# A two-block transformer forward pass on one core: query norm factors of the attention heads move into the exponential, squares of the low-rank parts are added on GpSimd, and sixteen modulation quarters move from TensorE to VectorE

## The reference, cut to what matters

```python
def rms(x, w):
    y = xf * lax.rsqrt(jnp.mean(xf * xf, axis=-1, keepdims=True) + EPS)
    return (y * w).astype(x.dtype)
...
qa = rms(heads(qa, H_A), qn_a)          # 8 heads of 64
ka = rms(heads(ka, H_A), kn_a)
qb = rms(heads(qb, H_B), qn_b)          # 12 heads of 64
kb = rms(heads(kb, HKV_B), kn_b)        # 4 heads of 64
qc = rms(heads(rms(cq, qa_norm) @ w_qb, H_C), qn_c)     # cq has 768 columns
kvc = heads(rms(ckv, kva_norm) @ w_kvb, H_C)            # ckv has 512 columns
...
qb, kb = apply_rope2d(qb, cos, sin), apply_rope2d(kb, cos, sin)   # latent tokens
...
s = einsum(q, k) * D ** -0.5 (+ bias for heads a, mask and sink for heads b)
p = softmax(s); o = p @ v
```

## Time and profile before

| what | value |
|---|---|
| median of 3 runs | 3268.7 us (3268.28 to 3268.73) |
| the profiled execution's own time | 3265.98 us |
| its span, first to last instruction | 3264.2 us |
| busy share PEld / DVE / ACT / POOL | 85% / 70% / 44% / 21% |
| DMA of the weight stream | 534.60 MB, queue 1 |
| FFN | about 810 to 1618 us |
| stages a0, za0, b0, zb0, c0 | from 1643, 1785, 1888, 2006, 2152 us |
| stages a1, za1, b1, zb1, c1 | from 2640, 2751, 2805, 2889, 2969 us |

### The profile page before, as it was taken

One profiled execution on the slowest core, in us unless ns is written; L12 is line 12 of the kernel. 1 busy time (PEld: TensorE's weight loads), 2 busy tenths in 40 slices (PEclk: granted clock), 3 DMA queues, 4 the chain that ended last, 5 costly groups with the idle time before them and its releaser, 6 DMA issues.

```text
span 3264.2 us, 56041 instructions
## 1 busy us (share of the span) xinstructions
PE 3220.0 (99%) x20212; PEld 2763.4 (85%) x20212; DVE 2299.4 (70%) x3399; ACT 1429.2 (44%) x2193; POOL 669.2 (21%) x600
## 2 busy tenths in 40 slices
PE   8999999999999999999999999999999999999999
PEld 8999999998998777889888777777878888888878
DVE  7887877567786776777766766566658776776765
ACT  5444445445444343444543433532352363543453
POOL 4999930111450000000300011000001100210000
PEclk9999999999999999999999999999999999999999
DMA  6555555565577777777733222134316553324435
GB/s 220 182 181 185 184 184 187 184 211 187 194 246 258 250 254 256 248 253 244 256 105 113 102 92 83 53 135 140 105 65 213 199 175 113 133 97 142 154 102 177
DMA packets 159873, 559.71 MB, mean 171 GB/s; under 512 B 17552, under 2 KB 23840, under 8 KB 159264
## 3 DMA queue, kind: packets, MB, share of 16 engines
q1 hardware_dynamic: 154144, 534.60, 48.1%
q0 software_dynamic: 5504, 22.04, 2.0%
HBM read 550.26 MB, written 6.31 MB: 171 GB/s over the span
## 4 chain that ended last, share of the span: by engine, by line
PE 89%; DVE 5%; ACT 2%; issue 1%; DVEq 1%; ACTq 0%; DMA 0%; POOL 0%; POOLq 0%; SPq 0%
PE psum L2168 17%; PE psum L2172 17%; PE psum L2169 17%; PE psum L2195 15%; PE psum L2196 7%; PE psum L2379 3%; PE psum L2521 2%; PE psum L2547 2%; PE psum L2532 2%; PE psum L2224 2%; PE psum L2380 2%; DVE wlo L1332 1%; PE psum L2299 1%; DVE rst L1363 1%; DVEq L1318 1%
## 5 line engine op out<-in xcount | busy, mean ns | idle before, releaser
L1332 DVE TENSOR_TENSOR wlo<-raw,whi 128x1024 fp32r<-128x1024 f32 (+3 forms) x844 | 1037.0, 1235 | 379.7 <-ACT whi L866 348.9
L866 ACT ACTIVATE whi<-raw 128x1024 fp32r<-128x1024 f32 (+3 forms) x844 | 863.3, 1029 | 949.9 <-PE psum L2172 465.3
L2168 PE MATMUL psum<-hcat,whi 128*128 128x256 f32 (+1 forms) x3436 | 1122.7, 327 | 4.9 <-DVE wlo L1332 4.2
L2172 PE MATMUL psum<-hcat,wlo 128*128 128x256 f32 (+1 forms) x3436 | 1109.4, 323 | 0.0
L2169 PE MATMUL psum<-hcat,whi 128*128 128x256 f32 (+1 forms) x3436 | 1109.3, 323 | 0.0
L2195 PE MATMUL psum<-hcat,whi 128*128 128x512 f32 x2048 | 724.2, 397 | 0.1
L2168 PEld LDWEIGHTS psum<-hcat,whi 128*128 128x128 f32 x3436 | 653.2, 190 | 72.9 <-issue 16.1
L2172 PEld LDWEIGHTS psum<-hcat,wlo 128*128 128x128 f32 x3436 | 653.1, 190 | 51.4
L2169 PEld LDWEIGHTS psum<-hcat,whi 128*128 128x128 f32 x3436 | 653.5, 190 | 49.4 <-issue 0.7
L2196 PE MATMUL psum<-hcat,wlo 128*128 128x256 f32 x2048 | 573.3, 280 | 0.0
L2195 PEld LDWEIGHTS psum<-hcat,whi 128*128 128x128 f32 x2048 | 384.3, 188 | 105.9 <-issue 17.2
(11 more groups left out here) (307 smaller groups left out, 3647.3 us busy)
## 6 DMA issues: line engine op xcount, KB each, us to landing
raw<-in_stream SPq DMA_DIRECT2D x978, 512.0 KB, 3.9
raw<-in_stream SPq DMA_DIRECT2D x18, 384.0 KB, 3.0
raw<-in_stream SPq DMA_DIRECT2D x24, 256.0 KB, 2.9
resid_dram<-X POOLq DMA_DIRECT2D x2, 2048.0 KB, 9.4
crow<-c_dram POOLq DMA_DIRECT2D x4, 1024.0 KB, 9.1
bias<-in_natten POOLq DMA_DIRECT2D x16, 256.0 KB, 2.9
X<-resid_dram POOLq DMA_DIRECT2D x4, 1024.0 KB, 6.2
raw<-in_stream SPq DMA_DIRECT2D x16, 192.0 KB, 2.4
```

Source lines behind the costliest of these rows:

```text
L866: act.activation(whi[:, c % HI_SLOTS, 0:n], raw[:, slot, 0:n], ACT.Copy).then_inc(hi_ready, 1)
L1332: vec.tensor_tensor(wlo[:, slot, 0:n], raw[:, slot, 0:n], whi[:, c % HI_SLOTS, 0:n].bitcast(F32), ALU.subtract).then_inc(lo_ready, 1)
L2168: pe.matmul(dst, h, cat[:, kk, c0:c0 + width], start=(q == 0 and k == 0), stop=False)
L2172: last = pe.matmul(dst, l_, cat[:, kk, c0:c0 + width], start=False, stop=(q == nq - 1 and k == nch - 1))
```

## The change

1. **Query factors.** The jobs of the query tiles of heads a and b are gone. Each query tile is squared once by ACT (`q_square`; for b straight from PSUM), and PE makes column sums with the square as the stationary side: 4 full float32 matmuls of two columns in layer 0, 2 in layer 1 (`qcol`, before tile t + 2). Once a stage, `q_factors` on DVE makes from all of them the factors for the exponential and for the maximum. The product of the gains of query and key goes into the keys (heads a); for heads b the query gain is applied as the tile leaves PSUM, which waits for ACT's square. Bias (heads a) is now scaled per head, two instructions instead of one; heads b have one small instruction more before the exponential. The key jobs stay, and the sum of layer 1's stage a stands one tile earlier.
2. **Rope of heads b** is done by DVE alone.
3. **Low-rank squares.** ACT squares one tile at a time, POOL adds them (`lora_adds`), and PE sums one source for ckv and two for cq.
4. **Modulation.** The last two FFN groups lose their eight quarters among the down tiles (`MOD_FEWER`): 16 quarters, two blocks. They come as rows of stage a0 (two beside each of tiles 0 to 3) and b0 (two beside tiles 0, 1, 4, 5). The second half of the vector is then loaded after the first four quarters of b0.

```diff
-MOD_GROUPS = [MOD_FEW] * FF_GROUPS
+MOD_FEWER = [0, 2] * 8 + [0] * KD
+MOD_GROUPS = [MOD_FEW] * 3 + [MOD_FEWER] * 2
...
-ROW_MODS = dict(a0=[0] * 10 + [1, 1], za0=[1] * 6, c0=[2, 2, 0, 2, 2, 2, 1, 1, 2, 1, 1])
+ROW_MODS = dict(a0=[2, 2, 2, 2, 0, 0, 0, 0, 0, 0, 1, 1], za0=[1] * 6, b0=[2, 2, 0, 0, 2, 2, 0, 0, 0, 0], c0=[2, 2, 0, 2, 2, 2, 1, 1, 2, 1, 1])
...
+            def heads_at(js, nq_):
+                for t in range(nq_):
+                    at_(t + 1, "qsq", t)
+                    at_(t + 2, "qcol", t)
+                    if name == "b":
+                        at_(t + 1, "rope", ROPES_OF[f"b{l}"][t])
+                at_(nq_ + 2, "qstat")
...
-                at_(4, "sq", ckv, 0, 4, 3)
-                at_(5, "sum", ckv, 0, 4)
+                for m in range(4):
+                    at_(m + 1, "part", ckv, m, l, m)
+                at_(5, "sum", ckv, 0, 1)
...
-                at_(9, "sq", cq, 0, 3, 7)
-                at_(10, "sum", cq, 0, 3)
-                at_(k0, "sq", cq, 3, 6, 10)
-                at_(k0 + 1, "sum", cq, 3, 6)
+                for m in range(6):
+                    at_(6 + m, "part", cq, m, l, 5 + m)
+                at_(k0, "sum", cq, 0, 1)
+                at_(k0 + 1, "sum", cq, 1, 2)
...
+            def q_factors(name, l):
+                k, nq_ = 2 * l + (name == "b"), Q_TILES[name]
+                st = q_mean(nq_, l)
+                nb = chunks_w(l) // P
+                vec.wait_ge(qsq_used, q_no(name, l, nq_))
+                sums_ = psum[:, 6, 0:8 * nq_].rearrange("p (h b) -> p h b", b=4)[:, :, 0:nb]
+                vec.tensor_scalar(st, sums_, 1.0 / HD, EPS, ALU.mult, ALU.add).then_inc(q_mean_ready, 1)
+                vec.wait_ge(q_root_ready, k + 1)
+                if name == "a":
+                    vec.tensor_scalar(q_inverse[:, :, :], st[:, :, 0:2], HD ** 0.5, None, ALU.mult)
+                    fence()
+                vec.reciprocal(st, st)
+                fence()
+                for dst, f in ((q_factor, HD ** -0.5), (q_minus, -HD ** -0.5)):
+                    vec.tensor_scalar(dst[:, 0:2 * nq_, 0:nb], st, f, None, ALU.mult)
+                fence()
...
-                    vec.scalar_tensor_tensor(ps[:, :, 0:S], bias[:, n % BIASES, :, :], 1.0 / u["scale"], ps[:, :, 0:S],
-                                             ALU.mult, ALU.add)
+                    for h in range(2):
+                        vec.scalar_tensor_tensor(ps[:, h, 0:S], bias[:, n % BIASES, h, :],
+                                                 q_inverse[:, 2 * u["c"] + h, u["q0"] // P:u["q0"] // P + 1],
+                                                 ps[:, h, 0:S], ALU.mult, ALU.add)
...
+                    elif it[0] == "qcol":
+                        name, t = "b" if first == T0[f"b{l}"] else "a", it[1]
+                        n = q_no(name, l, t)
+                        pe.wait_ge(qsq_ready, n + 1)
+                        for b in range(chunks_w(l) // P):
+                            last = pe.matmul(psum[:, 6, 8 * t + b:8 * t + b + 8:4], sq[:, n % 4, P * b:P * b + P],
+                                             halves[:, 0::HD], start=True, stop=True)
+                        last.then_inc(qsq_used, 1)
...
+            def lora_adds(l, name, j):
+                a0, adds = LORA_ADDS[name]
+                acc, w = jobs[j]["srcs"][0][0], jobs[j]["width"]
+                for m in range(1, adds + 1):
+                    a = 7 * l + a0 + m - 1
+                    pool.wait_ge(part_ready, 9 * l + (0 if name == "ckv" else 4) + m + 1)
+                    pool.tensor_tensor(acc, acc, sq[:, a % 2, 0:w], ALU.add)
+                    pool.drain().then_inc(part_used, 1)
+                pool.drain().then_inc(sq_ready, 1)
```

## The result

The changed kernel takes 3275.7 us (median), the kernel before 3268.2 us in the same rounds: ratio 1.0027, 95% interval 1.0019 to 1.0035. I had forecast 3254.2 us and a gain. The change makes the kernel slower by 0.27%, 21.5 us away from the forecast and outside the range.

What follows compares the result with a forecast made beforehand. The prediction took PE's own work, plus its waits, to bound the kernel. Its terms, -10.4 + 6.6 - 7.8 - 4.0 + 1.1 = -14.5 us, gave 3251.5 us, or 3254.2 us for a median, range 3248 to 3262 us.

Steps and rivals of the forecast that it cites:

- modulation taken from PE: FFN down tiles: eight pairs of quarters and two folds leave PE, 10.4 us less, bounds 0 and 10.4.
- the same quarters on DVE: Stages a0 and b0: 46 us of DVE time for 32 products, hidden behind PE's tiles, so 0; upper bound 46 us.
- column sums for query sums: Heads a and b, ten tiles a layer: column sums cost PE more than the sums replaced, 6.6 us more, bounds 0 and 13.
- waits of heads b gone: Heads b, both layers: PE's six waits before sums go, 5.4 us less.
- new waits before keys' sums: Tile 8 of b0: DVE's turn takes 12.8 us against PE's 11.4 us, 1.4 us more; in a0 it just fits.
- softmax chain: Heads a and b: chain from score to exponential some 0.25 us longer, 1.1 us more in total, bounds 0 and 4.
- low-rank sums, layer 0: Sums of 3 ckv and 4 cq sources gone, 1.0 us back as a longer wait in kvb0: -5.0 us.
- low-rank sums, layer 1: Sums of 3 ckv and 4 cq sources gone, part given back in c1: -2.8 us.
- So I give back 1.6 us: In c1, part of the removed low-rank sums returns because kvb waits for DVE's last piece of ckv; bounds 0 and 4.3.
- the FFN does not get shorter: Rival: down tiles of the last two groups paced by conversion, 10.4 us lost, 3264.6 us; chance 0.08.
- more is gained: Rival: column sums cost no more than the sums, nothing given back in c1: -19 us, 3249.6 us; chance 0.09.
- the slower one: Rival: DVE overflows in a0 and b0 in the turn with two quarters; all products exposed, 3300 us; chance 0.05.

Runs made afterwards that it cites:

- quarters put back: Changed kernel with the sixteen modulation quarters behind the down tiles of the last two FFN groups again, none moved to a0 and b0: 3283.9 us.
- factors earlier: Changed kernel with the query factors of heads a and b made one tile earlier: 3271.7 us, ratio 1.0015.
- later column sums: Changed kernel with the column sums of the first two query tiles of a1 one tile later on PE: 3269.0 us, ratio 1.0008.
- constant scale: Changed kernel with the exponentials of heads a and b scaled by a constant instead of a column of factors: 3275.5 us, ratio 1.0027.
- cq on PE: Changed kernel with the squares of cq in layer 1 summed by PE as before the change, without POOL's adds: 3274.0 us, ratio 1.0023.
- low-rank sums alone: Kernel before with only the low-rank sums changed, in both layers; queries, rotations and modulation as before: 3265.0 us, ratio 0.9989.
- the repairs: Changed kernel with a1's first two column sums a tile later, query factors a tile earlier, and layer 1's cq squares summed by PE: 3264.2 us.
- the quarters alone: Kernel before with only the sixteen modulation quarters moved and POOL's load of the vector's second half taken forward: 3277.7 us, ratio 1.0033.
- the repairs with later column sums: Changed kernel with the repairs, plus column sums of heads c, their read-outs and spreads one tile later in both kvb stages: 3260.9 us, ratio 0.9982.

## Why the prediction was wrong

Step by step, in us, with the sum by the account of starts:

| step of the prediction | predicted | measured | by |
|---|---|---|---|
| modulation taken from PE | -10.4 | -7.2 | both traces, quarters put back |
| the same quarters on DVE | 0 | 0 | quarters put back |
| column sums for query sums | +6.6 | +6.6 | both traces |
| waits of heads b gone | -5.4 | -5.3 | both traces |
| new waits before keys' sums | +1.4 | +4.6 | both traces; factors earlier, for 3.9 of it |
| first column sum of a1 | none seen | +5.5 | later column sums |
| softmax chain | +1.1 | +5.2 | constant scale, for 3.2 of it |
| low-rank sums, layer 0 | -5.0 | -3.5 | both traces |
| low-rank sums, layer 1 | -2.8 | +1.9 | cq on PE, low-rank sums alone |
| no half clock at 844 us | none seen | -1.5 | both traces |
| attention c, out0 | none seen | +0.6 | a longer wait for DVE's `ada_t`, for 0.5 of it |
| out1 | none seen | +1.6 | open |

The measured column adds up to 8.5 us, against 8.2 us between the spans; the rest is in steps too small to be told apart. The new waits are 3.3 us in b0 and 1.3 us in a0.

**The step that failed first is a wait I did not look for.** I counted what PE has to do and which DVE turns fill up, as "two sums are needed" says, and left ACT's queue out. ACT has 56% of idle time, but in the first tiles of a1 it is nearly full. In the stretch view of the kernel before it is busy for 6.49 of 8 us there, the fourth of the busy times:

```profile
2642.00:2650.00 8.00, 7.67 (x62) 7.28 (x61) 6.51 (x9) 6.49 (x11) 0.00 (x0) 1.00 0.52 187
```

A step that moves a consumer nearer to its producer is a change of its own, and the removed `lag` line said so. It cost 5.5 us, some 2 us of it through the clock.

**New wait: 1.4 us.** The turn was the right one, at tile 8 of b0. The term for the query factors was mis-sized: "seven steps at 0.17, 1.2" counted DVE's instructions and not the round trip to ACT, whose table load takes 1.28 us in the middle. With 2.5 us instead of 1.2 the turn is 14.1 us and the wait 2.7 us, near the 3.3 measured; a0, which "just fits" at 11.1 us, then has one of 1.0 us, near the 1.3 measured.

**Softmax.** The waits were placed rightly, but the chain, from the last score's start to the end of DVE's product, is 0.36 us longer for heads a (5.51 to 5.87 us in za1) and 0.42 us for heads b (5.84 to 6.26 us in zb1), instead of 0.25. With the constant scale 0.19 and 0.25 us remain: those are DVE's steps, as predicted. The other 0.17 us come from the two exponentials with a column as scale. That price stood in the trace of before, where heads c have the form (775 against 677 ns), and I did not look it up:

```profile
L1224 ACT ACTIVATE probs<-psum,stat,q_factor 128x512 f32<-128x512 f32 x24 | 18.4, 775 | 5.0 <-DVE stat L1964 4.9
```

With 0.4 us more the chain also gets late in zb0, where nothing waited before; there it costs 2.1 us. The Trainium skill (ScalarE: Activation LUTs, What ACT_TABLE_LOAD costs) gives 93 ns for each pointer operand of an activation; this case agrees, 770 - 677 and 556 - 463 ns.

**Low-rank sums.** The gross gain came as counted: 2.6 us for each three sources, in both layers. "So I give back 1.6 us" was the failure in layer 1. What came back is 4.7 us more than that (1.6 of it a half clock in kvb1), since without the sums PE's tile is shorter than the loop between DVE and ACT (6.46 us, 6.99 with POOL's add in it), so a good part of the sums had been free there. The earlier trace rows had it: DVE busy for 32.0 of 39.3 us with waits for ACT in between, and I read those waits as room; the turn of 6.46 us could be read in the trace of before. POOL's adds of 256 columns were mis-sized too: one shows 1.49 us where I took the 0.74 us of a product, but the rest of weights beside it is late by 0.53 us only. In layer 0 the wait in kvb0 grew from 1.9 to 2.8 us as predicted (1.0), and a half clock came with it.

**Modulation.** The down tiles of the fourth group do wait for DVE's rests of weights now, eight times. By the starts that is 3.0 us over the usual distance, and 3.6 us with the product behind each, which is slower too: all of the 3.2 us that are missing. The fifth group has no such wait. That is the rival "the FFN does not get shorter", for a third of the sum. In the timeline of the changed kernel the first product behind such a wait starts 0.90 us after the last one:

```profile
1438.50 0.28 PE L2252 MATMUL psum<-thirdcat,wlo 128*128 128x256 f32 x1
1439.40 0.36 PE L2248 MATMUL psum<-thirdcat,whi 128*128 128x256 f32 x1 [0.62 <-DVE wlo L1393]
```

**One rival was mis-added.** Column sums no dearer than the sums they replace are 6.6 us less, not the 3 us in "more is gained". That rival lies on the other side of the forecast, so nothing of the result hangs on it.

**What was right:** column sums at their price, the waits of heads b gone at theirs, free quarters in a0 and b0 and why (alone they cost 10 us), and a wait in the turn named. **What was wrong in kind:** of the corrections of more than 0.5 us all but one are losses, and that one, the missing half clock, is luck. A sum of gains at their upper end, in a kernel whose waits are spread over three engines, has its errors on one side, and my range left 8 us for them. None of the rivals held them, since the slower one bet on a single place.

By parts, from the medians of single kernels, good to some 2 us: low-rank sums -2.7 us; query factors with both of them +18.9 us (3283.9 - 3265.0); moved quarters -8.2 us. The kernels of 3265.0 and 3283.9 us, the low-rank sums alone and the quarters put back, share the slower pace between 717 and 805 us (last section), and the other two have the faster one, so the first and the last part may be off by 1.65 us each. With the repairs the query factors cost about as much as they let the quarters gain.

## What to carry to other kernels

Where PE is the bound, work taken from it counts only down to the pace of the loop behind it; time that loop, instruction by instruction with its waits on the partner engine, before counting the gain. When a diff shortens the distance between a producer and its consumer, write down the queue ahead of the producer at that point. A round trip between two engines is priced with the partner's table load, not by the instructions of one.

## What the runs showed of the hardware

- A wait of PE may cost more than itself, and whether it does is not in its length alone. Counted by starts of products, the 3.4 us pause in b0 was followed by a half clock in one of five profiled executions, the 3.0 us pause in kvb0 in seven of eight, the 2.5 us pause at 841 us in nine of twelve, and the 1.4 us pause in kvb1 in four of six. At half clock the starts of 256 columns follow at 0.21 instead of 0.12 us, and a stretch of 3.4 us costs some 1.6 us.
- A column as scale costs an exponential 93 ns, at 256 and at 512 elements.
- In out1 the distance between a product of 512 columns and the next of 256 is 230 ns in some kernels and 236 to 237 ns in others (230 before, with the quarters alone and with the low-rank sums alone; 236 to 237 in all kernels with query factors). It is 1.5 us in the stage, the clock is full, and its cause stays open.
- The same two paces stand between 717 and 805 us, where no kernel of this study differs from another: a stretch of this work takes 86.10 us in six of the twelve profiled executions (the kernel before, the changed one and the repairs with later column sums among them) and 87.75 us in the other six (the three repairs, the quarters put back and the low-rank sums alone among them), at full clock. So a difference of 1.65 us between two kernels may have nothing to do with their edits. Whether the pace belongs to a kernel or to one execution no run here shows.
